# Level products and state-times-query on four 32-column tiles in the recurrent heads of a hybrid decoder step

## What is computed

```
def hgrn_chunked(q, g, k, v, s0, chunk):        # 4 heads, key dim 128, value dim 128
    def step(S, inp):
        qc, gc, kc, vc = inp
        b = jnp.cumsum(gc, axis=1)
        dec = jnp.exp(jnp.where(tril, b[:, :, None] - b[:, None, :], -jnp.inf))
        att = jnp.einsum('btshk,bshk->bhts', qc[:, :, None] * dec, kc)
        o = jnp.einsum('bhts,bshv->bthv', att, vc) + jnp.einsum('bthk,bhkv->bthv', qc * jnp.exp(b), S)
        b_last = b[:, -1]
        S = jnp.exp(b_last)[..., None] * S + jnp.einsum('bshk,bshv->bhkv', kc * jnp.exp(b_last[:, None] - b), vc)
        return S, o
```

## Time and profile before

| what | value |
|---|---|
| median of the runs | 3167.92 us |
| span of the profiled execution | 3171.5 us |
| TensorE matmuls busy | 3027.7 us (95%) |
| VectorE busy | 2338.7 us (74%) |
| ScalarE busy | 1496.9 us (47%) |
| GpSimd busy | 1309.5 us (41%) |
| mean granted TensorE clock | 0.985 of full speed |

### The profile page before, as it was taken

How to read it: one execution, slowest core, us unless ns; L and a number is a source line. 1 busy time by engine, 2 the same in 40 slices (tenths; PEclk the granted TensorE clock), 3 DMA queues, 4 the chain that set the end, 5 groups by cost and what they waited for, 6 DMA issues and landing times. The chain is left out here.

```text
span 3171.5 us, 58263 instructions
## 1 busy us (share of the span) xinstructions
PE 3027.7 (95%) x23346; PEld 2878.9 (91%) x23346; DVE 2338.7 (74%) x2944; ACT 1496.9 (47%) x2652; POOL 1309.5 (41%) x745
## 2 busy tenths in 40 slices
PE   8999999999889999999999999999998899999997
PEld 8999879988779999999999998799886899999996
DVE  7877772734689999786677877636447999997866
ACT  6452463534545545553454434644444454555533
POOL 1111241012476777654511112411125767775644
PEclk9999999999989999999999999999999999999998
DMA  5112333304523434575421123332054333436654
GB/s 193 48 42 68 89 110 118 97 30 165 208 95 125 150 127 150 172 219 168 153 93 42 51 66 90 120 120 87 31 204 171 104 132 126 153 121 212 206 164 150
DMA packets 188523, 394.29 MB, mean 124 GB/s; under 512 B 13664, under 2 KB 113248, under 8 KB 185696
## 3 DMA queue, kind: packets, MB, share of 16 engines
q1 hardware_dynamic: 187968, 390.50, 37.4%
q10 hardware_dynamic: 288, 0.06, 0.0%
HBM read 307.41 MB, written 77.82 MB: 121 GB/s over the span
## 5 line engine op out<-in xcount | busy, mean ns | idle before, releaser
L345 PE MATMUL ps<-hh,w_hi 128*128 128x258 f32 (+3 forms) x4320 | 1333.0, 309 | 61.7 <-DVE hl L3114 27.5
L346 PE MATMUL ps<-hl,w_hi 128*128 128x258 f32 (+3 forms) x4320 | 1307.4, 303 | 0.0
L347 PE MATMUL ps<-hh,w_lo 128*128 128x258 f32 (+3 forms) x4320 | 1306.6, 302 | 0.0
L330 POOL TENSOR_TENSOR w_lo<-w_raw,w_hi 128x1024 fp32r<-128x1024 f32 x133 | 346.3, 2607 | 1349.4 <-ACT w_hi L322 1349.4
L345 PEld LDWEIGHTS ps<-hh,w_hi 128*128 128x128 f32 x4320 | 818.8, 190 | 84.3 <-issue 37.8
L346 PEld LDWEIGHTS ps<-hl,w_hi 128*128 128x128 f32 x4320 | 820.5, 190 | 2.9
L347 PEld LDWEIGHTS ps<-hh,w_lo 128*128 128x128 f32 x4320 | 819.7, 190 | 0.0
L2360 POOL TENSOR_TENSOR w_lo<-w_raw,w_hi 128x512 fp32r<-128x512 f32 (+1 forms) x168 | 244.7, 1460 | 220.5 <-ACT w_hi L2774 220.5
L2354 POOL TENSOR_TENSOR w_lo<-w_lo_f,w_hi 128x512 fp32r<-128x512 f32 x176 | 259.8, 1496 | 178.4 <-DVE w_lo_f L3143 156.2
L345 PE MATMUL ps<-Y_r,w_hi 128*128 128x258 f32 x1056 | 299.6, 284 | 7.3 <-POOL w_lo L2354 3.9
L346 PE MATMUL ps<-Y_r,w_hi 128*128 128x258 f32 x1056 | 300.3, 284 | 0.0
(11 more groups left out here) (405 smaller groups left out, 5592.0 us busy)
## 6 DMA issues: line engine op xcount, KB each, us to landing
w_raw<-in_w_stream SPq DMA_DIRECT2D x252, 512.0 KB, 3.5
gates<-f_c SPq DMA_DIRECT2D x44, 516.0 KB, 2.8
hl_f<-gates SPq DMA_DIRECT2D x32, 516.0 KB, 5.5
xT<-in_w_stream SPq DMA_DIRECT2D x32, 512.0 KB, 6.9
sums<-xT SPq DMA_DIRECT2D x16, 1024.0 KB, 6.0
w_raw<-sums SPq DMA_DIRECT2D x64, 256.0 KB, 3.8
w_raw<-in_w_stream SPq DMA_DIRECT2D x48, 256.0 KB, 3.9
out_y_cols<-xT SPq DMA_DIRECT2D x6, 1376.0 KB, 9.2
```

Of the source, the lines that this page charges most:

```text
L330: nc.gpsimd.tensor_tensor(w_lo[:, SLOT[m], :], w_raw[:, m % RR, :], w_hi[:, SLOT[m], :].bitcast(F32), ALU.subtract).then_inc(lo_done["pool ...
L345: nc.tensor.matmul(out, whi, mhi, start=start, stop=False, skip_group_check=reopened)
L346: nc.tensor.matmul(out, whi, mlo, start=False, stop=False, skip_group_check=reopened)
L347: return nc.tensor.matmul(out, wlo, mhi, start=False, stop=stop, skip_group_check=reopened)
```

## The change

For levels 1 to 5 the diagonal blocks of 32 tokens are multiplied instead of those of 64: four matmuls for each chunk, each with 32 stationary and 16 moving columns, with outputs on partitions 0 to 31, 32 to 63, 64 to 95 and 96 to 127. Level 6 still needs blocks of 64 and stays as it is (`max(32, 1 << lv)`). The outputs lie in the same columns of the same bank as before, so `take` and the mask are the same. The product of the samples' states and queries is cut into four column blocks of the state, each a matmul of its own with 32 stationary columns.

```
+                def quarter(j):
+                    return slice(32 * j, 32 * j + 32)
@@ level
-                                for h in range(2):
-                                    own = X[lv % 3][:, P * c + HP * h:P * c + HP * h + HP]
-                                    at = HP * c + HP // 2 * h
-                                    last = nc.tensor.matmul(later_half(ps[HP * h:HP * h + HP, level_bank(lv), at:at + HP // 2], lv),
+                                w = max(32, 1 << lv)
+                                for h in range(P // w):
+                                    own = X[lv % 3][:, P * c + w * h:P * c + w * h + w]
+                                    at = HP * c + w // 2 * h
+                                    last = nc.tensor.matmul(later_half(ps[w * h:w * h + w, level_bank(lv), at:at + w // 2], lv),
                                                             own, halves(own, lv, 1), start=True, stop=True)
@@ samples
                         for b in range(NS):
-                            last = nc.tensor.matmul(ps[:, BC, 256 + b:257 + b], E[:, P * b:P * b + P],
-                                                    Q[r % 2][:, SEQ + b:SEQ + b + 1], start=True, stop=True)
+                            for j in range(4):
+                                last = nc.tensor.matmul(ps[quarter(j), BC, 256 + b:257 + b], E[:, P * b + 32 * j:P * b + 32 * j + 32],
+                                                        Q[r % 2][:, SEQ + b:SEQ + b + 1], start=True, stop=True)
```

## The result

The changed kernel takes 3148.6 us (median of four, 3147.1 to 3150.4) and the kernel before 3168.5 us beside it (3167.8 to 3172.3): a ratio of 0.9933, interval 0.9921 to 0.9944. That is 19.9 us or 0.67% faster. Forecast were 3144.5 us, and 3139 to 3158 as the range.

What follows compares the result with a forecast made beforehand. TensorE was taken to bound the heads. Savings of 16.9 us (levels 1 to 5) and 7.7 (samples' product), less 1.2 lost in the last heads, made 23.4: 3167.9 to 3144.5 us, range 3139 to 3158.

Steps and rivals of the forecast that it cites:

- What bounds the heads: In the eight heads TensorE sets the time; what is taken off it comes off the end until another engine is late.
- The step of 128 and 64 columns: TensorE's present steps: 0.112 us for 128 columns, 0.058 for a pair of 64, following the weights' width, not the moving columns.
- The step of 32 columns: On TensorE, a group of four 32-column passes takes 0.032 us, with 0.029 as the lower end.
- The upper end: A group of four 32-column passes takes what a pair takes now, 0.058 us, or more; 3163.5 us, chance 0.08.
- the rival of slower groups: Groups of four run slower than their loads, 0.045 us each, in levels and samples' product: 3153.7 us, chance 0.11.
- Levels 1 to 5: Each level's passes take 0.51 us for 0.93, saving 0.42; five levels in eight heads save 16.9 us.
- The samples' product: Its passes take 0.51 us for 1.79; less 0.31 for changing width, 0.97 saved a head, 7.7 us in eight.
- the new change of width: Switching tile width around the samples' product, formerly between 128-column work, costs 0.31 us, bounds 0.21 and 0.62.
- No loss in heads 0 to 2: VectorE stays ahead of TensorE there, though 0.7 us short at the outputs (1054), having waited 0.81 us itself before.
- The rival in which VectorE takes over there: At 1054 VectorE's state chain comes no earlier, so six heads lose 0.7 us each: 3148.7 us, chance 0.08.
- The last heads: In each layer's last head, a chain from GpSimd's `w_lo` to `snew` loses 0.85 and 0.38 us, together 1.2.
- The rival on the slower side: Each pass costs TensorE's sequencer 0.029 us, so levels lose 0.93 each: 3208.4 us; break-even 0.016; chance 0.08.

Runs made afterwards that it cites:

- levels_only: The changed kernel with the samples' product back on 128 columns, levels 1 to 5 still on four tiles: 3156.8 us beside 3171.5 before the change.
- samples_only: The changed kernel with levels 1 to 5 back on blocks of 64 tokens, samples' product still on four tiles: 3164.2 us beside 3171.5 before the change.
- samples_64: The changed kernel with the samples' product on two tiles of 64 columns instead of four of 32: 3153.9 us (one run).
- after_again: The changed kernel, unaltered, run and profiled once more: 3148.0 us beside 3170.2 for the kernel before, ratio 0.9931.
- chunks_reversed: The changed kernel with the chunks of levels 1 to 5 taken from 7 down to 0: 3153.3 us (one run).
- levels_twice: The changed kernel with each of levels 1 to 5 computed twice into the same place, 128 passes in a row: 3171.5 us (one run).
- tile_by_tile: The changed kernel with the loops of levels 1 to 5 turned, all eight chunks of one tile before the next tile: 3191.9 us (one run).
- more_tiles: The changed kernel with 32-column tiles also in level 0 (heads 1 to 3) and levels 6 and 7: 3143.8 us beside 3170.2 before the change.

## Why the prediction was right

**What bounds the heads: right.** Each piece taken off TensorE came off the end, 2.89 us a head in heads 0 to 2, and the cuts of single pieces add up (levels_only, samples_only).

**The step of 128 and 64 columns: right.** That the time follows the width of the weights and not the moving columns was read from two products. samples_64 shows it within one product, with 1.01 us.

**The step of 32 columns: right.** 0.032 us for a group of four was taken. A level's eight first groups follow after 31.7 ns, the later ones after 33.4. The upper end, 0.058, and with it the rival of slower groups, is out: with it 64 loads would have spanned 0.8 us or more, and they span 0.64.

**Levels 1 to 5: the mechanism right, the term too large by 1.4 us.** 0.42 us was the saving of a level and 0.385 was measured, in the middle heads. Of the 0.035 missing 0.02 is in the passes: 64 x 8.3 ns = 0.53 us, where 16 x 0.032 = 0.51 stood. Another 0.01 is the long step behind load 33; the rest is rounding. So 15.4 instead of 16.9 us, before losses.

**The samples' product: right.** 0.97 us a head was the term; 0.95 (samples_only) and 0.96 (levels_only against the kernel after) were measured, about 7.7 us as forecast. The choice of 0.31 for the new change of width, between 0.21 and 0.62, held, though the idle time in it is 0.12 us and not 0.21.

**No loss in heads 0 to 2: right.** The worry was 1054 behind VectorE's chain over the states. The timelines of head 1, VectorE and then TensorE (its lines are now 1421 and 1059):

```profile
178.20 2.65 DVE L1421 SCALAR_TENSOR_TENSOR hg_work<-hg_work,hg_blast,ps 128x128 f32<-128x128 f32 x7
...
182.02 0.60 PE L1059 MATMUL ps<-hg_work,hg_vrows 128*128 128x128 f32 x4
```

The states are ready at 180.85 and TensorE comes at 182.02: 1.17 us of room, where the earlier trace rows had 2.4. VectorE gave up its wait of 0.81 us, as the forecast said, and kept ahead. But the forecast's reckoning was too tight: 2.4 of room, 0.8 given back and 2.9 saved would have left 0.3 us. Its states come 4.86 us earlier, of which 0.3 is the heads' earlier start and 2.9 head 0, so 1.7 us are gained within head 1, twice the 0.81. The rest comes from VectorE's waits for the level products, 2.9 us in this head before and 1.1 after. The rival in which VectorE takes over there (3148.7 us) has the right total by chance; the wait it needs is not there.

**The last heads: right in the place, wrong in the split.** 0.85 us in layer 0 and 0.38 in layer 1 were to be lost, 1.2 together. Against the 2.89 of a middle head the last ones gave 2.67 and 2.53 us, so 0.6 was lost in the first execution. In after_again 1.9 and 1.5 were gained and 2.4 lost; in chunks_reversed, whose levels take the same time, 2.6 and 1.7, with 1.5 lost. The forecast's 1.2 lies within these, and that is partly luck, for the step that set it was too simple. It took the moment at which GpSimd and SyncE start the chain as what moves. It moves with them, and on top of it the landing of the swapped rows varies: from before to after SyncE issued them 303.81 - 293.69 = 10.12 us earlier, but VectorE's rotation came 313.94 - 303.25 = 10.69 us earlier; in after_again it was 10.29 and 10.13. Hence also the wait of 1043 (now 1047) of 0.6 us in the first execution instead of the 1.4 forecast: 0.54 + 2 x 0.385, less 0.57 for the quicker landing and 0.16 for what the next paragraph shows. The wait of 0.4 us forecast for layer 1 is not in the first execution's list; after_again has one of 0.7 there.

A piece of it that the forecast did not have: level 5 of the last heads gives 0.24 us and not 0.385 (its usual share is 0.40). The kernel after, timelines of GpSimd, VectorE and PEld, layer 0:

```profile
289.94 2.40 POOL L330 TENSOR_TENSOR w_lo<-w_raw,w_hi 128x1024 fp32r<-128x1024 f32 x1 [5.90 <-ACT w_hi L322]
...
290.04 2.85 DVE L1281 TENSOR_TENSOR hg_work<-xT 128x512 f32<-128x512 f32 x1
292.92 0.69 DVE L1282 TENSOR_TENSOR hg_work<-xT 128x512 f32<-128x512 f32 x1
293.53 0.93 DVE L1252 TENSOR_TENSOR Y<-ps,rs 128x344 f32<-128x344 f32 x2
...
293.27 0.64 PEld L977 LDWEIGHTS ps<-xT 128*32 128x32 f32 x64 [0.21 <-issue]
294.09 0.19 PEld L345 LDWEIGHTS ps<-hh,w_hi 128*128 128x128 f32 x1 [0.18 <-DVE Y L1252]
```

The unit behind the level waits 0.18 us for the read-out of an earlier unit. VectorE is late with it because its operation on line 1281 took 2.85 us there, against 0.69 for its twin on 1282. It began while GpSimd's `w_lo` was running (289.94 to 292.34) and ended 0.55 us after it. This is no single case: of the 112 operations on lines 1281 and 1282, the 17 that begin while a `w_lo` runs take 2.7 to 2.9 us, and each ends 0.55 us after it; the other 95 take 0.68 to 0.73. The kernel before has the same 17 (2.2 to 2.9 us) and 95. That GpSimd's operation holds VectorE's back is read from these 34 cases; no run moves `w_lo` away to test it. VectorE ended 0.55 us after `w_lo` at this place before as well (2.46 us on line 1276); what is new is that TensorE, with shorter levels 4 and 5, comes soon enough to wait. The forecast that the read-outs hang on TensorE and move with it was true wherever VectorE had room, and not here. Two such places cost 0.3 us.

**The rival on the slower side, a price for each pass: out.** levels_twice puts it at 8.3 ns or less; 16 was the point from which the change would have lost. The estimate of 1.6 us for the 64 passes of a level, which stands beside this rival, is out with it: they take 0.53. tile_by_tile shows, though, what such a rival would have looked like: with a level's passes 27 ns apart on average, 3191.9 us.

**The sum.** 15.4 + 7.7 - 0.6 = 22.5 us by the measured terms, as in the heads; 23.4 were forecast. The measured time is 4.1 us over the forecast's 3144.5: 0.9 of it is this difference, 0.6 is that the kernel before took 3168.5 us beside the changed one and not 3167.9, and 2.6 is what the heads show beyond the medians (22.5 for 19.9 us). The ratio's interval means 18 to 25 us, and the second set of runs gives 22.2, so the 2.6 us are within the uncertainty of the medians. Nothing here assigns them, or the 3.6 beyond the heads in the span, to a line.

## What to carry to other kernels

Small fp32 products with few moving columns should be cut into 32-column blocks of their weights and handed out to the four tiles in turn, chunk outside and tile inside. This pays where the weights had 64 columns (the levels: twice the matmuls took 0.64 us for 1.01, and with the other nesting 1.80) and more so where they had all 128 (the samples' product: 0.63 us for 1.87). Expect the gain only as long as a tile's weight load is the longer side; with 64 moving columns (level 7) it had all but ended, in the one case tried. Add the change of width (0.3 us) wherever the product stands between work over all 128 columns, and before counting the saving in full, look for a chain whose start is a DMA.

## What the runs showed of the hardware

- **Pace.** Four tiles of 32 columns take an fp32 pass each 8.3 ns on average, over 128 passes in a row in 37 of 40 rows (levels_twice), and 8.2 to 8.6 ns over 64 passes with 1, 16 or 32 moving columns. One tile alone takes one each 31 to 32 ns (tile_by_tile), and two tiles of 64 columns a pair each 58 ns.
- **Two patterns.** The first 32 loads of a level begin in groups of four every 31.7 ns, the later ones in twos every 16.7 ns, with one step of 22 ns behind load 33; the pattern goes by place in the row (chunks_reversed), and the twos go on to load 128 in 37 of 40 rows (levels_twice).
- **Loads and moving columns.** On two tiles, pairs of passes with 32 stationary columns begin 56 ns apart with 64 moving columns and 32 ns apart with 32 (more_tiles, levels 7 and 6).
- **VectorE beside GpSimd.** An operation on lines 1281 and 1282 that begins while GpSimd's `w_lo` runs takes 2.7 to 2.9 us and ends 0.55 us after it, 17 of 17 times in the kernel after; the 95 others take 0.68 to 0.73 us.
- **One program, two executions.** The DMA ahead of VectorE's rotation landed 0.56 us later against the start of the span in one execution than in the other (0.7 us later against its own issue, and against the start of the heads), and the last head took 0.7 us longer.
